# Row products of a hybrid encoder block: one bank at a time, or four banks in turn

## The reference, cut to what matters

```
h = rmsnorm(x, norm1_g)
z = h @ w_in + b_in          # mq, mk, mv, mo, mi, mf, fq, fk, fv, ff, gm, gf
mq, mk = silu(causal_depthwise_conv([mq, mk]))
hm = mlstm_chunkwise(mq, mk, mv, mi, logsigmoid(mf));  y_m = norm(hm) * g * sigmoid(mo)
hf = forgetting_attention(fq, fk, fv, logsigmoid(ff)); y_f = hf
mix = sigmoid(gm) * (y_m @ w_br_mlstm) + sigmoid(gf) * (y_f @ w_br_fox)
x = x + mix @ w_out
x = x + (silu(h2 @ w_gate) * (h2 @ w_up)) @ w_down    # h2 = rmsnorm(x, norm2_g), D_FF = 2816
out = rmsnorm(x, norm_f_g)
```

## Time and profile before

| | |
|---|---|
| runs of the kernel before | 819.29, 819.95, 820.02 us, median 819.95 |
| span of the profiled execution (first to last instruction) | 818.3 us; the page gives no other time of it |
| PE busy | 805.7 us (98%), 3851 MATMULs |
| PEld busy | 652.7 us (80%) |
| DVE, ACT, POOL busy | 371.3, 255.4, 24.0 us |
| mean granted TensorE clock | 0.997 of full speed |
| value projections, output's first half, down (start us) | 66.96, 404.89, 692.31 |

### The profile page before, as it was taken

The page is one execution under the profiler, slowest core; times in us unless marked ns, Lnnn a source line. Parts: engine busy times, 40 slices in busy tenths (PEclk is TensorE's granted clock), DMA queues, the critical chain, the costliest instruction groups (busy, mean ns, idle before and its releaser), DMA issues.

```text
span 818.3 us, 9506 instructions
## 1 busy us (share of the span) xinstructions
PE 805.7 (98%) x3851; PEld 652.7 (80%) x3851; DVE 371.3 (45%) x573; ACT 255.4 (31%) x421; POOL 24.0 (3%) x43
## 2 busy tenths in 40 slices
PE   6999999999999999999999999999999999999996
PEld 6988887888665578888888988888888888888885
DVE  4688334357654443424435534434443443323224
ACT  6444211343433323323324333322333223213211
POOL 4000000012000000000000000000000000000001
PEclk9999999999999999999999999999999999999999
DMA  8434342311010103533331333322233332331402
GB/s 225 126 99 145 103 129 77 103 52 31 22 52 1 52 1 103 206 103 103 103 103 52 92 115 103 103 89 80 90 102 103 104 103 83 123 103 52 155 0 103
DMA packets 61915, 75.63 MB, mean 92 GB/s; under 512 B 3680, under 2 KB 49840, under 8 KB 61872
## 3 DMA queue, kind: packets, MB, share of 16 engines
q1 hardware_dynamic: 61872, 75.02, 28.9%
HBM read 72.92 MB, written 2.10 MB: 92 GB/s over the span
## 4 chain that ended last, share of the span: by engine, by line
PE 94%; DMA 2%; DVE 1%; issue 1%; ACT 1%; SPq 0%; POOL 0%; POOLq 0%; ACTq 0%; DVEq 0%
PE bank L1136 27%; PE bank L1138 27%; PE bank L1137 27%; PE bank L1319 3%; PE bank L1339 3%; PE bank L1260 2%; DMA x_nat<-in_x 1%; PE bank L1327 1%; PE bank L1299 1%; DMA stage<-in_w_in 1%; PE bank L1286 1%; DVE work L783 0%; DVE w_lo L722 0%; PE bank L1279 0%; PE bank L1148 0%
## 5 line engine op out<-in xcount | busy, mean ns | idle before, releaser
L1136 PE MATMUL bank<-hT_hi,w_hi 128*128 128x512 f32 (+1 forms) x680 | 261.6, 385 | 2.7 <-DVE hT_lo L706 2.5
L1138 PE MATMUL bank<-hT_hi,w_lo 128*128 128x512 f32 (+1 forms) x680 | 257.1, 378 | 0.0
L1137 PE MATMUL bank<-hT_lo,w_hi 128*128 128x512 f32 (+1 forms) x680 | 257.0, 378 | 0.0
L722 DVE TENSOR_TENSOR w_lo<-stage,w_hi 128x1024 fp32r<-128x1024 f32 x125 | 152.4, 1224 | 223.0 <-ACT w_hi L464 214.3
L464 ACT ACTIVATE w_hi<-stage 128x1024 fp32r<-128x1024 f32 x127 | 133.3, 1052 | 132.8 <-PE bank L1138 125.5
L1136 PEld LDWEIGHTS bank<-hT_hi,w_hi 128*128 128x128 f32 x680 | 128.9, 190 | 26.1 <-POOL w_lo L407 2.8
L1138 PEld LDWEIGHTS bank<-hT_hi,w_lo 128*128 128x128 f32 x680 | 128.7, 189 | 23.7
L1137 PEld LDWEIGHTS bank<-hT_lo,w_hi 128*128 128x128 f32 x680 | 128.8, 189 | 21.6
L1136 PE MATMUL bank<-w_hi,aT_hi 128*128 128x512 f32 x176 | 68.5, 389 | 0.0
L1137 PE MATMUL bank<-w_lo,aT_hi 128*128 128x512 f32 x176 | 68.5, 389 | 0.0
L1138 PE MATMUL bank<-w_hi,aT_lo 128*128 128x512 f32 x176 | 68.5, 389 | 0.0
(11 more groups left out here) (169 smaller groups left out, 821.3 us busy)
## 6 DMA issues: line engine op xcount, KB each, us to landing
stage<-in_w_in SPq DMA_DIRECT2D x21, 1024.0 KB, 5.2
stage<-in_w_gate SPq DMA_DIRECT2D x11, 1024.0 KB, 5.3
stage<-in_w_up SPq DMA_DIRECT2D x11, 1024.0 KB, 5.3
stage<-in_w_down SPq DMA_DIRECT2D x22, 512.0 KB, 4.4
stage<-in_w_out SPq DMA_DIRECT2D x4, 1024.0 KB, 5.0
x_nat<-in_x SPq DMA_DIRECT2D x4, 512.0 KB, 5.4
stage<-in_w_br_mlstm SPq DMA_DIRECT2D x4, 512.0 KB, 3.5
stage<-in_w_br_fox SPq DMA_DIRECT2D x4, 512.0 KB, 4.6
```

Source lines behind the costliest of these rows:

```text
L722: dve.tensor_tensor(ring(w_lo, g), staged(g), ring(w_hi, g).bitcast(F32), ALU.subtract).then_inc(lo_split, 1)
L1136: pe.matmul(o, a_hi, b_hi, start=first, stop=False)
L1137: pe.matmul(o, a_hi, b_lo, start=False, stop=False)
L1138: return pe.matmul(o, a_lo, b_hi, start=False, stop=last)
```

## The change

The loops over row blocks that called `row_product` are replaced by calls of a new helper, `four_rows`. For each of the two depths of a granule it issues the hi*hi MATMULs of the four row blocks, each into its own bank, then the four hi*lo, then the four lo*hi. The number of MATMULs, their operands and their shapes stay; the order changes, and with it the bank from one MATMUL to the next. In the value projections the four takes of the first granule now all stand before its first MATMUL.

```diff
+            def four_rows(g, banks, src_hi, src_lo, k0, first, last):
+
+                wh, wl = ring(w_hi, g), ring(w_lo, g)
+                for k in range(2):
+                    opens, closes = first and k == 0, last and k == 1
+                    for r in range(ROWS):
+                        pe.matmul(psum[banks[r]][:, :], src_hi[:, k0 + k, r * P:(r + 1) * P], wh[:, k, :],
+                                  start=opens, stop=False)
+                    for r in range(ROWS):
+                        pe.matmul(psum[banks[r]][:, :], src_hi[:, k0 + k, r * P:(r + 1) * P], wl[:, k, :],
+                                  start=False, stop=False)
+                    for r in range(ROWS):
+                        ins = pe.matmul(psum[banks[r]][:, :], src_lo[:, k0 + k, r * P:(r + 1) * P], wh[:, k, :],
+                                        start=False, stop=closes)
+                return ins
+
@@ value projections
                     for r in range(ROWS):
                         if d == 0:
                             take(V_BANKS[n][r], (v_ready, ROWS * n + r + 1))
-                        last = row_product(g0 + d, V_BANKS[n][r], r, hT_hi, hT_lo, 2 * d, d == 0, d == 3)
+                    last = four_rows(g0 + d, V_BANKS[n], hT_hi, hT_lo, 2 * d, d == 0, d == 3)
                     last.then_inc(used, 1)
@@ first half of the output projection
-                for r in range(ROWS):
-                    last = row_product(G_OUT + d, 4 + r, r, mixT_hi, mixT_lo, 2 * d, d == 0, d == 3)
+                last = four_rows(G_OUT + d, (4, 5, 6, 7), mixT_hi, mixT_lo, 2 * d, d == 0, d == 3)
                 last.then_inc(used, 1)
@@ down
-                    for r in range(ROWS):
-                        last = row_product(g, bank0 + r, r, aT_hi, aT_lo, 2 * d, d == 0, d == D_GRAN - 1)
+                    last = four_rows(g, range(bank0, bank0 + ROWS), aT_hi, aT_lo, 2 * d, d == 0, d == D_GRAN - 1)
                     last.then_inc(used, 1)
```

## The result

| | before | after |
|---|---|---|
| median of 20 runs each, us | 819.96 | 821.78 |
| lowest to highest | 818.75 to 821.45 | 820.73 to 822.21 |
| profiled execution: span, us | 818.3 | 819.0 (its own time 820.92) |
| down's first to last MATMUL start, us | 119.45 | 119.45 |

A forecast was written before the change was run, and what follows sets the result against it. PE, busy for 98% of the span, was taken to bound the kernel. Bank order 0, repeated stationary tile 0 and the value projections' takes 1.64 us, added to 819.95, gave 821.6 us, range 820.0 to 823.4.

The forecast's parts named there:

- The order of banks: Value projections, output projection and down: 600 more changes of bank change the time by -0.2 to +0.3 us, taken as 0.
- The stop at bank 4: Start of value projections: PE waits for ACT's copy of block 7, first start 68.47 instead of 66.96 us, 1.51 us.
- The restart: First distances after PE's stop at the value projections run below full pace: 0.13 us more.
- Nothing gives it back: From 66.96 us to the end PE has no other wait, so the 1.64 us stays in the total.
- the line of 0.2%: Smallest change a measurement of this kernel can tell from no change, 1.64 us; slower beyond it 0.51, within it 0.44.
- the signposts in absolute time: Profile after: first row product starts near 68.5 us, and down's start moves from 692.31 to about 693.95 us.
- The faster pitch: Rival: 13.3 ns per MATMUL come from adding into the same bank; 8.0 us saved, 813.6 us; chance 0.05.
- The clock didn't fall: Rival: the new stop lowers the clock for 3.3 us, about 1.6 us more lost, 823.2 us; chance 0.09.
- The change of bank at every MATMUL starves nothing: Answers the rival that rotation breaks PE's dense run: all 720 at lower clock, 144 us more, about 965 us; chance 0.01.
- no change: Rival: the wait is taken back by later slack on PE or never stands, time stays 819.95 us; chance 0.08.

The follow-up runs named there:

- the second experiment: Changed kernel with value projections put back to old order and takes; output's first half and down stay rotated: 819.96 us, ratio 0.9999.
- the smaller dose: Kernel before, with only the takes for the second, third and fourth bank together before the first granule's second row block: 820.13 us, ratio 1.0002.

## Why the prediction was right, point by point

**The order of banks is worth nothing.** Forecast from two mean distances and one change of bank; shown by down's 119.45 us in both kernels and by the two kernels that rotate without the early wait. The bound of -0.2 to +0.3 us for all 720 was fair: over the 528 rotated MATMULs of the output projection and down, and the rows of the second experiment agree within 0.02 us.

**The stop at bank 4.** Forecast 1.51 us, measured 1.60 us. The term that was mis-sized is the time from the reader's end to PE's start. The prediction took 0.05 us from one wait for DVE's `w_lo`; here it is 0.15 us (67.52 - 67.37), 0.14 in the kernel with the takes alone and 0.15 in the smaller dose, always behind ACT's copy. It isn't a sum of 0.05 us over waits in a row, since the dose has three waits and pays the same as four. Nor is it simply a matter of which engine is waited for. Here are two other waits in the profile after:

```profile
12.64 0.68 DVE L706 TENSOR_TENSOR hT_lo<-bank,hT_hi 128x512 fp32r<-128x512 f32 x1
...
13.42 0.36 PE L1136 MATMUL bank<-hT_hi,w_hi 128*128 128x256 f32 x1 [1.62 <-DVE hT_lo L706]
...
36.21 1.22 DVE L722 TENSOR_TENSOR w_lo<-stage,w_hi 128x1024 fp32r<-128x1024 f32 x1
...
37.48 0.50 PE L1136 MATMUL bank<-hT_hi,w_hi 128*128 128x512 f32 x1 [0.86 <-DVE w_lo L722]
```

Both are for DVE, and they give 13.42 - 13.32 = 0.10 us and 37.48 - 37.43 = 0.05 us. So the prediction took the shortest of the three kinds. What sets this time stays open.

**The restart.** Forecast 0.13 us, measured 1.72 - 1.60 = 0.12 in the changed kernel and 1.68 - 1.59 = 0.09 with the takes alone.

**Nothing gives it back.** The 1.72 us are still there at down's start, and the medians differ by 1.82 us; the interval of the ratio is 1.1 to 2.1 us and holds both. The measured ratio, 1.0020, lies on the line of 0.2% between slower and within, as the prediction said of its forecast; on which side of that line a measurement falls, the mechanism does not decide.

**What was read wrongly** are the signposts in absolute time: a first row product near 68.5 and down's start near 693.95. They came at 67.52 and 692.98, though the mechanism was as described, since the opening took about 1 us less in that execution. In the six profiles of fp32r kernels block 7's last MATMUL starts anywhere from 65.69 to 66.92 us. In five of them the distance from there to the end of its copy is 1.68 or 1.69 us (68.42 - 66.74, 67.37 - 65.69, 68.60 - 66.92 and 67.63 - 65.94, for instance).

**Where the forecast was lucky.** The sixth, of the kernel with the rotation alone, has 67.91 - 66.49 = 1.42 us:

```profile
36.74 1.22 DVE L722 TENSOR_TENSOR w_lo<-stage,w_hi 128x1024 fp32r<-128x1024 f32 x1
...
38.19 0.39 PE L1138 MATMUL bank<-hT_hi,w_lo 128*128 128x512 f32 x1
38.41 0.39 PE L1136 MATMUL bank<-hT_hi,w_hi 128*128 128x512 f32 x1
...
67.24 0.67 ACT L501 ACTIVATE z_pad<-bank,vec 128x512 f32<-128x512 f32 x1
```

In the other five PE waits near 38 us for this `w_lo` and restarts 0.05 to 0.06 us behind it, which ties PE to the chain of DVE and ACT. In the sixth it comes 0.45 us behind `w_lo` (38.41 - 37.96) and doesn't stop, so it pays no restart either: against the copy it is 0.45 - 0.05 - 0.13 = 0.27 us later, and 1.68 - 1.42 is 0.26. The copy ends 29.94 or 29.95 us after this `w_lo` in the profiles of before, after and the sixth. So the size of the stop depends on the opening of the execution. Had the four takes stood ahead in the sixth, the stop would have been about 0.26 us shorter (an estimate from these two distances). The profile that the forecast was read from happened to be of the common kind; the prediction doesn't name this condition.

**The rivals.** The faster pitch would have needed 2.7 ns at each change of bank; down has 360 more of them after the change and takes the same time to 0.01 us, so nothing of 0.1 ns is seen. The clock didn't fall: the granted clock is 1.00 from 66 to 72 us, with 1.43 us idle. In the opening of the profile before it was 0.50 from 15.0 us on, behind a stop of 2.5 us. In the profile after, the stop at the same place of the opening is 1.6 us, and the clock stays at 1.00 behind it:

```profile
14.00:18.00 4.00, 3.97 (x34) 3.73 (x33) 2.84 (x6) 3.97 (x8) 0.83 (x2) 1.00 0.54 117
```

What decides between the two was not tried. The change of bank at every MATMUL starves nothing: no stop and a clock of 1.00 in down.

**Two slips in the prediction's numbers** that the forecast doesn't rest on. Its range of 820.0 to 823.4 us is said to hold all rivals but the last two, but the 819.95 us of "no change" lies just below it. And the 0.99 to 1.72 us called the part outside the first and last instruction are three runs against the span of one execution. In the 20 runs of the changed kernel, where each has its own span, that part is 1.9 to 2.1 us. It cancels, since the 1.64 us were added to the median.

## What to carry to other kernels

Before an order of work is changed, look at what its old order hid: here eighteen MATMULs into free banks stood in front of the one bank that wasn't free, and a helper that opens all four banks at once made PE wait for the slowest of them. Where a helper must open several outputs together, let the first piece run one output after the other, with the bank that comes free last at its end; the kernel with its first granule as before does this and loses nothing. And whether "neighbouring products into one bank" cost anything can be read before a line is written, from the distance between starts at a change of bank and from the means of two stretches that change banks at different rates.

## What was not expected of the hardware

The time from the end of what PE waited for to PE's start is not one number: 0.14 to 0.15 us behind the ACT copy of line 501, 0.10 us behind DVE's line 706, 0.05 us behind DVE's line 722. An fp32r product of 512 columns takes 226.7 ns from start to start with a weight load of 188 ns, a bf16 one (with a fixed stationary tile) 215.8 ns with a load of 98 ns. And 360 more changes of bank in a dense stretch of 528 MATMULs moved its 119.45 us by no more than 0.01 us.
